# Prompt attention moved into the compression of a hybrid decoder layer

## The reference, cut to what matters

```
kc, vc = compress_rows(rows of the cmp cache and of the prompt)   # gelu(blk @ w1) @ w2, 16 rows a step
prompt:  o_A  = softmax over its own rows (three dilated windows folded into one mask), 8 heads
         o_B  = gate*cmp + gate*sel + gate*win, 8 heads on 2 KV heads
sample:  p_cmp = softmax(q @ kc)
         imp   = p_cmp @ overlap, summed over the heads of a group
         idx   = top-16 of 17 blocks of 64 rows (one block of those not forced drops out)
         o_B   = gate*cmp + gate*selected + gate*win over paged caches; o_A over a cache of 1024 rows
```

## Time and profile before

| | |
|---|---|
| median of 3 runs | 1454.82 us (1453.14 to 1455.51) |
| profiled execution | 1458.25 us, span 1456.2 us |
| mean granted clock of TensorE | 0.958 |
| projection | 0 to 111.4 us |
| compression | 111.4 to 253.6 us |
| prompt attention and choice of blocks | 253.6 to 348.6 us |
| sample loop | 348.6 to 498.9 us |
| routing | 498.9 to 694.9 us |
| experts | 694.9 to 1456.2 us |

### The profile page before, as it was taken

How to read it: one execution, slowest core, us unless ns; L and a number is a source line. 1 busy time by engine, 2 the same in 40 slices (tenths; PEclk the granted TensorE clock), 3 DMA queues, 4 the chain that set the end, 5 groups by cost and what they waited for, 6 DMA issues and landing times.

```text
span 1456.2 us, 26137 instructions
## 1 busy us (share of the span) xinstructions
PE 1364.6 (94%) x8712; PEld 1136.4 (78%) x8712; DVE 943.7 (65%) x2189; ACT 526.6 (36%) x1002; POOL 289.1 (20%) x491
## 2 busy tenths in 40 slices
PE   9989998787898899999999999999999999999996
PEld 6869988554554536778899898989989898998985
DVE  4440000676444232998999788888888888888876
ACT  4410001453223202111333445454544545454453
POOL 0112221310000011764112112121212222222201
PEclk9989999698889998999999999999999999999998
DMA  7876876801678712526698599989999999999972
GB/s 255 294 274 232 301 263 235 315 1 66 210 295 320 278 60 89 183 77 190 194 271 249 180 320 316 314 311 309 318 318 319 316 307 308 317 316 322 313 223 83
DMA packets 157468, 359.03 MB, mean 247 GB/s; under 512 B 50514, under 2 KB 92178, under 8 KB 153682
## 3 DMA queue, kind: packets, MB, share of 16 engines
q1 hardware_dynamic: 126258, 241.21, 49.6%
q0 software_dynamic: 24512, 110.84, 21.5%
q10 hardware_dynamic: 6624, 6.03, 1.3%
HBM read 341.82 MB, written 53.35 MB: 271 GB/s over the span
## 4 chain that ended last, share of the span: by engine, by line
PE 47%; DVE 3%; issue 1%; DVEq 1%; ACT 0%; POOLq 0%; POOL 0%
PE psum L1574 24%; PE psum L1564 6%; PE psum L1563 6%; PE psum L1562 6%; PE psum L1587 2%; PE psum L1106 2%; DVE gated_i L1718 2%; DVEq L1718 0%; DVE OT L1714 0%; DVE ln_bn L1046 0%; DVE products L1723 0%; DVE x L1041 0%; DVE v_lo L1731 0%; DVE x L1061 0%; DVE gated_lo L1767 0%
## 5 line engine op out<-in xcount | busy, mean ns | idle before, releaser
L1564 PE MATMUL psum<-x_hi,u_lo 128*128 128x256 f32 x760 | 215.1, 283 | 0.0
L1563 PE MATMUL psum<-x_lo,u_hi 128*128 128x256 f32 x760 | 215.0, 283 | 0.0
L1562 PE MATMUL psum<-x_hi,u_hi 128*128 128x256 f32 x760 | 214.6, 282 | 0.0
L1731 DVE TENSOR_TENSOR v_lo<-big,v_hi 128x1024 fp32r<-128x1024 f32 x128 | 156.8, 1225 | 33.8 <-ACT v_hi L1642 33.8
L1642 ACT ACTIVATE v_hi<-big 128x1024 fp32r<-128x1024 f32 x128 | 135.2, 1057 | 84.9 <-PE psum L1574 82.5
L1574 PE MATMUL psum<-v_hi,gated_hi 128*128 128x512 f32 x512 | 160.0, 394 | 4.3 <-DVE gated_lo L1767 4.3
L1574 PE MATMUL psum<-v_lo,gated_hi 128*128 128x512 f32 x512 | 159.0, 391 | 0.0
L1574 PE MATMUL psum<-v_hi,gated_lo 128*128 128x512 f32 x512 | 158.5, 391 | 0.0
L1563 PEld LDWEIGHTS psum<-x_lo,u_hi 128*128 128x128 f32 x760 | 145.5, 191 | 3.7
L1562 PEld LDWEIGHTS psum<-x_hi,u_hi 128*128 128x128 f32 x760 | 145.5, 191 | 3.7
L1564 PEld LDWEIGHTS psum<-x_hi,u_lo 128*128 128x128 f32 x760 | 145.5, 191 | 0.0
(11 more groups left out here) (302 smaller groups left out, 2407.8 us busy)
## 6 DMA issues: line engine op xcount, KB each, us to landing
big<-in_peer_v SPq DMA_DIRECT2D x128, 512.0 KB, 4.7
big<-in_peer_u SPq DMA_DIRECT2D x116, 512.0 KB, 5.0
big<-in_a_k SPq DMA_DIRECT2D x8, 2048.0 KB, 11.9
a_vals<-in_a_v SPq DMA_DIRECT2D x8, 2048.0 KB
keep_ak<-in_a_k POOLq DMA_DIRECT2D x32, 508.0 KB, 6.1
keep_av<-in_a_v POOLq DMA_DIRECT2D x24, 512.0 KB, 6.4
sel_pages<-in_sel_pool SPq DMA_DIRECT2D x64, 128.0 KB, 2.9
wq_ring<-in_peer_wq SPq DMA_DIRECT2D x16, 512.0 KB, 3.9
```

What stands on the lines that cost most here:

```text
L1562: pe.matmul(H[:, 0:SEQ], uh[:, q, kc], x1h[:, k, :], start=(k == 0), stop=False)
L1563: pe.matmul(H[:, 0:SEQ], uh[:, q, kc], x1l[:, k, :], start=False, stop=False)
L1564: mm = pe.matmul(H[:, 0:SEQ], ul[:, q, kc], x1h[:, k, :], start=False, stop=(k == KD - 1))
L1731: ve.tensor_tensor(vl[:, q], vs[:, q], vh[:, q].bitcast(F32), ALU.subtract).then_inc(s["v_lo"], 1)
```

## The change

1. Prompt attention leaves `attention_block` and runs in `compress_block`. Its 36 steps are spread over 24 slots: one behind each half h of `hidden(u)` for u = 2 to 13, slots of one and of two steps in turn. All engines put the steps into their order at that place. On ACT a slot stands behind the gelu of the half. On DVE the result of `second` is copied before the slot of h = 1.
2. PSUM is divided anew: banks 0 and 1 one half each of the first layer, 2 the second layer, 3 and 4 scores (both heads in one bank), 5 and 6 turned weights, 7 the values of all kinds. The wait before the first product of A or cmp is for 2g or 2g+1 copies out.
3. The units of samples 6 and 7 come in the order key 6, key 7, value 6, value 7. In the last two units (NK = 14 on) the sample blocks are scored: `block_scores`, `block_turn`, `block_sums`, `head_sums` on PE, `block_weights` and `importance` on DVE. `choose()` (maximum, index, penalty) runs on DVE in iteration 0 of the sample loop.
4. SP waits for whole pairs of units before it loads pages, and loads a_k of sample 0 after the pages of sample 3, w_k of samples 0 and 1 after those of sample 4. The other loads of the samples begin with `attention_block`, as before.
5. Keep copies 0 to 15 leave the projection and go into the first eight units of the routing on POOL, two each behind `onehot_ids`.
6. Some tiles share memory (`t.mid`) that the projection used for rotated rows.

```diff
-            for u in range(16, 4 * nblk):
-                gp.wait_ge(s["w_lo"], u + 1)
-                for x in range(2):
-                    keep_copy(gp, d, s, 2 * (u - 16) + x)
...
+        units = [(b, a) for b in range(NB - 2) for a in range(2)] + [(b, a) for a in range(2) for b in (NB - 2, NB - 1)]
+        NK = len(units) - 2
+        STEPS = NU + 4
+        SLOTS = 2 * (NK - 2)
+        def prompt_steps(u, h):
+            j = 2 * (u - 2) + h
+            if not 0 <= j < SLOTS:
+                return range(0)
+            return range(STEPS * j // SLOTS, STEPS * (j + 1) // SLOTS)
...
+            for b in range(2, NB):
+                sp.wait_ge(s["cmp_hid"], 4 * (b - 1))
+                load_cmp_pages(sp, t, d, s, b % 2, b * PAGES)
+                if b == 3:
+                    sp.dma_start(t.big[:, 0:4 * PAST].rearrange("p (c n) -> p c n", c=4), d.a_k[0]).then_inc(s["ld_ka0"], 16)
+                if b == 4:
+                    for x in range(2):
+                        sp.dma_start(t.kw[:, x], d.w_k[x]).then_inc(s[f"ld_ka{x}"], 16)
...
+            def hidden(u, h, part=range(CMP_W1)):
...
+                if u and part[0] == 0:
+                    pe.wait_ge(s["cmp_gelu"], 2 * (u - 1) + h + 1)
...
+            def p_pv(u):
+                i, c, k = PUNITS[u]
+                n, nk, kr = prompt_shape(u)
+                pe.wait_ge(s["p_turned_out"], u + 1)
+                g = u // 4
+                if k == "cmp" or g and k == "A":
+                    pe.wait_ge(s["p_OT"], 2 * g + (k == "cmp"))
...
+            def prompt(u, h):
+                for v in prompt_steps(u, h):
+                    if v == 0:
+                        pe.wait_ge(s["cmp_done"], 1)
+                    if v == 3:
+                        pe.wait_ge(s["cmp_done"], 2)
+                    if v < NU:
+                        p_scores(v)
+                    if 2 <= v < NU + 2:
+                        p_turn(v - 2)
+                    if 3 <= v < NU + 3:
+                        p_pv(v - 3)
...
+            for u in range(len(units)):
+                hidden(u, 0)
+                if u == NK:
+                    second(u - 1)
+                    block_scores()
+                if u == NK + 1:
+                    block_turn()
+                prompt(u, 0)
+                if u == NK + 1:
+                    hidden(u, 1, range(CMP_W1 // 2))
+                    block_sums()
+                    hidden(u, 1, range(CMP_W1 // 2, CMP_W1))
+                    head_sums()
+                    second(u - 1)
+                else:
+                    hidden(u, 1)
+                    if 1 <= u < NK:
+                        second(u - 1)
+                prompt(u, 1)
+            second(len(units) - 1)
...
+            def prompt(u, h):
+                for v in prompt_steps(u, h):
+                    if v < NU:
+                        p_exp(v)
+                    if 2 <= v < NU + 2:
+                        p_out(v - 2)
+                    if v >= 4 and PUNITS[v - 4][2] in ("A", "win"):
+                        p_OT(v - 4)
+            for u in range(len(units)):
+                gelu(u, 0)
...
+                prompt(u, 0)
...
+                gelu(u, 1)
+                prompt(u, 1)
...
                 gp.tensor_tensor(pi[:, q].rearrange("p h k n -> p h n k"), eq[:, q], ci[:, q].unsqueeze(3).broadcast_to([P, 2, NPAIR, TOPK]), ALU.mult).then_inc(s["id_mul"], 1)
+                if u < 8:
+                    for x in range(2):
+                        keep_copy(gp, d, s, 2 * u + x)
```

More of the change, by code:

```diff
@@ L350, in load_cmp_pages @@
                       d.cmp_pool[bass.ds(r, 1)].rearrange("a p n -> p (a n)")).then_inc(s[f"cmp_pg{slot}"], 16)
[L353 to L463, removed]
@@ L469, with prompt_shape, prompt_queries @@
+KINDS = ["A", "cmp", "sel", "win"]
+PUNITS = [(i, c, k) for i in range(2) for c in range(4) for k in KINDS]
+NU = len(PUNITS)
+def prompt_shape(u):
+    i, _, k = PUNITS[u]
+    return (NC_P, 1, NC_P) if k == "cmp" else (P * (i + 1), i + 1, P)
+def prompt_queries(u):
+    return 3 * (u // 4) + min(u % 4, 2)
 NKA, NKW = PAST + NT, 512 + NT
@@ L529, in attention_block @@
         bank = lambda i: t.psum[:, i]
[L530 to L537, removed]
-        def queries(u):
-            return 3 * (u // 4) + min(u % 4, 2)
-        last_reader = lambda x: 4 * (x // 3) + (0, 1, 3)[x % 3]
         chunk = lambda b, n: 6 * b + n
@@ L552, in _ @@
                     sp.wait_ge(s["s_scores"], chunk(b - 2, 3) + 1)
-                sp.dma_start(ka[:, q], d.a_k[b]).then_inc(s[f"ld_ka{q}"], 16)
-                sp.dma_start(kw[:, q], d.w_k[b]).then_inc(s[f"ld_ka{q}"], 16)
+                if b >= 1:
+                    sp.dma_start(ka[:, q], d.a_k[b]).then_inc(s[f"ld_ka{q}"], 16)
                 if b >= 2:
+                    sp.dma_start(kw[:, q], d.w_k[b]).then_inc(s[f"ld_ka{q}"], 16)
                     sp.wait_ge(s["s_sel_used"], b - 1)
@@ L594, in _ @@
         @block.tensor
         def _(pe):
-            def p_scores(u):
-                i, c, k = units[u]
-                n = shape(u)[0]
-                if u >= 2:
-                    pe.wait_ge(s["p_masked"], u - 1)
-                pe.wait_ge(s["p_q"], queries(u) + 1)
-                keys = {"A": TT[:, KA0 + c, 0:n], "cmp": t.kc[:, NB, 0:min(n, NC_P)], "sel": TT[:, KS0, 0:n], "win": TT[:, KW0, 0:n]}[k]
-                for e in range(2):
-                    mm = pe.matmul(bank(2 * (u % 2) + e)[:, 0:n], qd[:, queries(u) % 4, e, :], keys, start=True, stop=True)
-                mm.then_inc(s["p_scores"], 1)
@@ L607, in p_turn @@
-            def p_turn(u):
-                n, nk, kr = shape(u)
-                pe.wait_ge(s["p_weighed"], u + 1)
-                if u >= 2:
-                    pe.wait_ge(s["p_turned_out"], u - 1)
-                for e in range(2):
-                    for x in range(nk):
-                        mm = pe.transpose(bank(4 + u % 2)[0:kr, (2 * e + x) * P:(2 * e + x + 1) * P], pp[:, u % 4, e, x * P:x * P + kr], ident)
-                mm.then_inc(s["p_turned"], 1)
-            def p_pv(u):
-                i, c, k = units[u]
-                n, nk, kr = shape(u)
-                pe.wait_ge(s["p_turned_out"], u + 1)
-                g = u // 4
-                if g and k in ("A", "cmp"):
-                    pe.wait_ge(s["p_OT"], 2 * g - (k == "A"))
-                for x in range(nk):
-                    for e in range(2):
-                        v = {"A": hk[:, x, (2 * c + e) * HD:(2 * c + e + 1) * HD], "cmp": t.vc[0:min(kr, NC_P), NB, e * HD:(e + 1) * HD],
-                             "sel": hk[:, x, HK_VS + e * HD:HK_VS + (e + 1) * HD],
-                             "win": hk[:, x, HK_VW + e * HD:HK_VW + (e + 1) * HD]}[k]
-                        mm = pe.matmul(bank(6 + (k != "A"))[e * HD:(e + 1) * HD, 0:P], v, pT[0:kr, u % 2, 2 * e + x, :],
-                                       start=(x == 0 and k in ("A", "cmp")), stop=(x == nk - 1 and k in ("A", "win")), skip_group_check=True)
-                mm.then_inc(s["p_pv"], 1)
@@ L634, in _ @@
-            for u in range(NU + 3):
-                if u < NU:
-                    p_scores(u)
-                if 2 <= u < NU + 2:
-                    p_turn(u - 2)
-                if u >= 3:
-                    p_pv(u - 3)
-            pe.wait_ge(s["diag"], 12)
-            for b in range(NB):
-                mm = pe.matmul(bank(0)[0:64, b * NC_S:(b + 1) * NC_S], qn[:, 0, b, :], t.kc[:, b, :], start=True, stop=True)
-            mm.then_inc(s["i_mm"], 1)
-            pe.wait_ge(s["i_pc"], 4)
@@ L906, in _ @@
-            for u in range(NU + 1):
-                if u < NU:
-                    p_mask(u)
-                if u == 8:
-                    sample_queries()
-                if u >= 1:
-                    p_weigh(u - 1)
-            ve.wait_ge(s["p_pv"], NU)
-            over = lambda z: z.unsqueeze(2).broadcast_to([64, NB, NC_S])
-            ve.wait_ge(s["i_mm"], 1)
-            ve.tensor_scalar(pc[:].rearrange("p b n -> p (b n)"), bank(0)[0:64, 0:NB * NC_S], SCALE, None, ALU.mult).then_inc(s["i_dve"], 1)
@@ L926, in _ @@
-            ve.wait_ge(s["i_dve"], 3)
-            ve.tensor_tensor(pc[:], pc[:], over(cst[:, 1]), ALU.mult).then_inc(s["i_pc"], 1)
-            ve.wait_ge(s["i_mm"], 3)
-            ve.tensor_copy(x1[:], bank(2)[0:64, 0:NB * NSEL]).then_inc(s["i_pc"], 1)
-            ve.wait_ge(s["i_mm"], 4)
-            ve.tensor_scalar(imp[:], bank(7)[0:64, 0:NB * NSEL].rearrange("p (b j) -> p b j", j=NSEL)[:, :, 14:0:-1], -1.0, None, ALU.mult).then_inc(s["i_sel"], 1)
-            ve.wait_ge(s["i_sel"], 1)
-            for b in range(NB):
-                ve.max(top[:, b], imp[:, b]).then_inc(s["i_sel"], 1)
@@ L944, in _, with choose @@
-            ve.wait_ge(s["i_sel"], 3 + 2 * NB)
-            ve.tensor_scalar(pen[:, :, 1:15], pen[:, :, 1:15], NEG, None, ALU.mult).then_inc(s["i_pen"], 1)
-            ve.wait_ge(s["i_pen"], 1)
+            def choose():
```

(16 more changed lines are left out.)

449 lines of the change are left out of this document (301 added, 148 removed).

## The result

The changed kernel takes 1483.11 us (1480.51 to 1486.57, 4 runs) against 1454.24 (1453.14 to 1455.51, 4 runs): ratio 1.0186, 95% interval 1.0158 to 1.0215. It is slower, by 29 us; 1476 was forecast. The profiled execution took 1485.07, with a span of 1483.0.

A forecast was written before the change was run, and what follows sets the result against it. PE was taken to bound the compression, engine-to-engine latency the prompt attention, transfers the sample loop. Projection -4.5, compression +108, sample loop -83, routing +1 gave +21 on the median 1454.82: 1476 us, range 1450 to 1492.

The forecast's parts named there:

- no waits for pages: Compression: four waits for pages and the slow clock behind one should go, -8.5 us with small remainders.
- +1 in the routing: Routing: the moved copies on POOL stay hidden except in the first unit, +1 us (0 to 6).
- Bank waits: Compression: PE waits at the values product for ACT's copy-out, 15 x 3.0 = 45 us (15 x 2 to 15 x 3.6).
- Clock: Compression: products following 13 of the new waits run slower, 0.7 us each, 9 us (0 to 20).
- Steps: Compression: PE work of the prompt attention steps coming in, 52 us (45 to 66).
- Double slots: Compression: in 12 slots of two steps, second-step turn and values wait for DVE's weighing and ACT's copy, 5 us.
- Compression in all: Whole compression stretch: -8.5 + 52 + 45 + 5 + 9 + 5.5 = +108 us.
- Projection: Projection: without 16 cache copies weights come in time, -4.5 us (-5 to 0).
- Sample loop, T + 162: Output projection starts 162 us (150 to 170) after T, SP's load start in the block, against 245.4 before: -83.
- first rival: Compression: copy-out waits about 1 us and no clock fall, so faster at 1437 us; chance 0.13.
- third rival: Effects cancel: waits of 2.4 us, no clock loss, 3 us less in the sample loop, 1455 us; chance 0.07.
- second rival: Compression: a table switch holds ACT twice the 1.28 us, with a drain; +38 us, 1513 us; chance 0.07.

The follow-up runs named there:

- copy-out first: Changed kernel with the copy-out of the values bank put ahead of the exponential in the same ACT step: 1431.9 us, ratio 0.9836 to the kernel before.
- no gelu: Changed kernel with the compression's gelu replaced by an identity, so no table loads between exponentials: 1483.5 us, ratio 1.0191 to the kernel before.
- copies back: Changed kernel with keep copies 0 to 15 in the projection again, not in the routing: 1488.1 us, ratio 1.0193 to the kernel before.
- no early loads: Changed kernel with a_k of sample 0 and w_k of samples 0 and 1 issued at the sample loop's start: 1481.9 us, ratio 1.0186.

## Why the prediction was right

It forecast slower, by a mechanism, its place and its count, and these hold: 15 waits at the values product for the copy-out, 46 table loads, no waits for pages, +1 in the routing. What was off are sizes, and some of them cancelled: that the compression came out within 3 us of its forecast is in part luck.

- Bank waits, +45: measured 37.1. The round from scores to values was 4.39 us (269.72 to 274.11) with 256 columns, 4.7 assumed. I had put a gelu's table load into each slot's chain; it is issued right after the last copy-out (273.98), under the half product, so only the exponential's load stands in it. And with 128 columns the wait is 1.8 to 2.5, not the same 3, because DVE's two passes are 0.42 each instead of 0.69 and ACT's turned copy 0.36 instead of 0.57.
- Clock, +9 (bounds 0 and 20): measured 26. This is the term most wrongly sized, outside its own bounds. The halves alone lost 19.7 us, not 9: the clock fell at ten of the twelve slots with bank waits, whose halves took 5.2 to 6.5 us, about 2 us more each instead of 0.7. The other 6.6 us are the prompt's own products behind the gaps, which I had left out.
- Steps, +52: 49.5, as a remainder. Double slots, +5: 1.7, since a bank wait stands in most of them. It became 7.5 when the bank waits went.
- Compression in all +108, measured +110.9: 8 us too much for the waits and 17 too little for the clock, the rest in the small terms.
- Projection, -4.5: -6.2 here, 4 to 7 over all executions; what it is worth in the whole kernel's time is not resolved. Sample loop, T + 162: T + 166.7, within the scatter of a loop that is bound by transfers, and inside 150 to 170.
- The first rival (waits near 1 us, 1437) did not occur as the code stands; "copy-out first" brings its short waits about, by ACT's order and not by early scores: 1432.
- The third rival had the waits nearly right (2.4 us, measured 37.1 / 15 = 2.5) and failed by the clock: it allowed no loss, and 26 us came.
- The second rival, a switch at twice the load's time, is excluded. The exponential at 159.65 starts 0.02 us after a load that began at 158.35 and took 1.28; the load began right behind the gelu:

```profile
157.97 0.37 ACT L638 ACTIVATE cmp_hidden<-psum,cmp_bias 128x126 f32<-128x126 f32 x1 [3.73 <-PE psum L487]
158.35 1.28 ACT L613 ACT_TABLE_LOAD   x1
159.65 0.40 ACT L613 ACTIVATE p_weights<-p_weights,att_negmax 128x128 f32<-128x128 f32 x1
```

The Trainium skill, "ScalarE: Activation LUTs", section "What ACT_TABLE_LOAD costs", would have a drain on top of the load; this trace shows none (0.02 us from the end of the load to the exponential, 0.01 from the gelu to the load), and without any load the time was the same (1483.5 us).

## What to carry to other kernels

When work is woven into another engine's stream, write down for each wait in which step of the other engine its release stands and what is ahead of it there: a release that needs this step's own first product costs most of a round, each time (2.9 of 4.4 us here with 256 columns). Move a copy-out to the first place where its input is ready before giving it a bank of its own; either cured this. A gap costs its own length and, behind ten of the twelve slots here, the clock of what follows: 37 us of gaps took 26 more, so filling them with idle products is a quick test of how much of a loss is clock. The better cure is to remove the gap: by the place of the copy-out at the bank, by steps spread evenly at the turns. Spreading was tried only on top of the other.

## What was not expected of the hardware

The length of a gap alone did not set the clock. In the changed kernel gaps of 2.51 and 2.49 us (before 197.72 and 212.20) were followed by half products of 3.84 us at a granted clock of 1.00, while one of 1.81 (before 187.44) was followed by one of 6.48 at 0.56. Behind gaps of 2.9 us the next half product always took 5.17 us or more, also where a step stood between. The two that kept the clock are the only waits with 128 columns in slots of one step; all others under 2.9 us stand in slots of two steps. The same two slots kept it in the three other kernels with this order on ACT and nothing in the gaps ("no gelu", "copies back", "no early loads"), so it is not the chance of one execution. Why was not tried.
